# Three edits to a ten-stage transformer kernel on one core: the input's load, the close of the convolutions, and the squares of the neighbourhood attention

## The reference, cut to what matters

```python
x = first_block(x, ...)            # "mix" (two attentions) and a convolutional feed-forward
for i in range(4):                 # mixers: conv, nat, ret, conv
    h = rmsnorm(x, norm1_g[i])
    x = x + mixer_i(h)
    h = rmsnorm(x, norm2_g[i])
    x = x + conv_ffn(h, ...)

def conv_module(h, w_in, b_in, dw_w, dw_b, ln_g, ln_b, w_out):
    a, gt = jnp.split(h @ w_in + b_in, 2, axis=-1)
    u = a * jax.nn.sigmoid(gt)
    u = dwconv(u, dw_w, dw_b)      # depthwise, 31 taps
    u = layernorm(u, ln_g, ln_b)
    return jax.nn.silu(u) @ w_out

# nat_mixer: per head of 64 features
q = rmsnorm(qkv[:, :, 0], q_g) * (NAT_HEAD_DIM ** -0.5)
k = rmsnorm(qkv[:, :, 1], k_g)
```

## Time and profile before

| what | value |
|---|---|
| median of 3 runs | 1642.3 us (1642.21 to 1643.4) |
| the profiled execution, its own time | 1641.51 us |
| its span | 1639.4 us |
| PE busy | 1609.6 us (98%), 10544 matmuls |
| DVE busy | 1223.5 us (75%) |
| ACT busy | 897.9 us (55%) |
| POOL busy | 68.7 us (4%) |
| chunk 0's first matmul | at 11.61 us |
| last transposes of conv0, first matmul of its output chunk | 411.17 and 414.58 us |
| nat: first matmul of chunk 0, last sum of squares | 629.21 and 687.37 us |

### The profile page before, as it was taken

One profiled execution on the slowest core, in us unless ns is written; L12 is line 12 of the kernel. 1 busy time (PEld: TensorE's weight loads), 2 busy tenths in 40 slices (PEclk: granted clock), 3 DMA queues, 4 the chain that ended last, 5 costly groups with the idle time before them and its releaser, 6 DMA issues.

```text
span 1639.4 us, 28560 instructions
## 1 busy us (share of the span) xinstructions
PE 1609.6 (98%) x10544; PEld 1458.4 (89%) x10544; DVE 1223.5 (75%) x1842; ACT 897.9 (55%) x1178; POOL 68.7 (4%) x77
## 2 busy tenths in 40 slices
PE   8999999999999999999999999999999999999998
PEld 8888999978899998888999998877999987799997
DVE  5766878778687877865877786446787887878787
ACT  5575554565655546575554555444645556664553
POOL 0041000000000000020000033000100000000000
PEclk9999999999999999999999999999999999999999
DMA  7444545443655454422545455533554545345443
GB/s 287 132 152 166 205 167 194 176 162 121 238 190 187 179 204 151 158 104 103 201 160 194 188 181 192 192 128 140 182 201 182 181 178 180 135 150 202 180 181 126
DMA packets 41889, 284.13 MB, mean 173 GB/s; under 512 B 4992, under 2 KB 5120, under 8 KB 8928
## 3 DMA queue, kind: packets, MB, share of 16 engines
q1 hardware_dynamic: 39552, 273.90, 45.7%
q0 software_dynamic: 2272, 9.32, 1.6%
HBM read 282.16 MB, written 1.05 MB: 173 GB/s over the span
## 4 chain that ended last, share of the span: by engine, by line
PE 88%; DVE 8%; ACT 2%; issue 1%; DMA 1%; DVEq 0%; SPq 0%; ACTq 0%
PE bank L1863 15%; PE bank L1865 15%; PE bank L1864 15%; PE bank L1957 8%; PE bank L1958 8%; PE bank L1959 8%; PE bank L1909 4%; PE bank L1910 4%; PE bank L1911 4%; DVE w_lo L1057 1%; DVE arena L1338 1%; PE bank L2018 1%; DMA raw<-wstream 1%; PE bank L1845 1%; PE bank L2283 1%
## 5 line engine op out<-in xcount | busy, mean ns | idle before, releaser
L1863 PE MATMUL bank<-h_hi,w_hi 128*128 128x256 f32 x2220 | 636.3, 287 | 4.8 <-DVE w_lo L1057 2.6
L1864 PE MATMUL bank<-h_hi,w_lo 128*128 128x256 f32 x2220 | 630.8, 284 | 0.0
L1865 PE MATMUL bank<-h_lo,w_hi 128*128 128x256 f32 x2220 | 630.7, 284 | 0.0
L1863 PEld LDWEIGHTS bank<-h_hi,w_hi 128*128 128x128 f32 x2220 | 426.2, 192 | 12.1 <-issue 6.2
L1864 PEld LDWEIGHTS bank<-h_hi,w_lo 128*128 128x128 f32 x2220 | 426.2, 192 | 4.4 <-issue 1.4
L1865 PEld LDWEIGHTS bank<-h_lo,w_hi 128*128 128x128 f32 x2220 | 426.2, 192 | 0.8
L1365 DVE TENSOR_TENSOR w_lo<-raw,w_hi 128x2048 fp32r<-128x2048 f32 x145 | 327.6, 2285 | 1.6 <-ACT w_hi L797 1.6
L1057 DVE TENSOR_TENSOR w_lo<-raw,w_hi 128x2048 fp32r<-128x2048 f32 (+3 forms) x110 | 237.4, 2158 | 111.8 <-ACT w_hi L585 111.8
L785 ACT ACTIVATE arena<-arena,par 128x256 f32<-128x256 f32 x220 | 120.4, 595 | 358.0 <-DVE arena L1324 354.7
L797 ACT ACTIVATE w_hi<-raw 128x2048 fp32r<-128x2048 f32 x150 | 286.1, 1907 | 19.7 <-PE bank L1959 19.7
L1957 PE MATMUL bank<-w_hi,h_hi 128*128 128x512 f32 x632 | 248.1, 393 | 3.3 <-DVE h_lo L1663 1.8
(11 more groups left out here) (206 smaller groups left out, 1327.2 us busy)
## 6 DMA issues: line engine op xcount, KB each, us to landing
raw<-wstream SPq DMA_DIRECT2D x254, 1024.0 KB, 4.8
arena<-window_bias POOLq DMA_DIRECT2D x4, 768.0 KB, 7.3
arena<-dilated_bias POOLq DMA_DIRECT2D x8, 256.0 KB, 5.1
arena<-conv_rows POOLq DMA_DIRECT2D x2, 1024.0 KB, 4.8
raw<-wstream SPq DMA_DIRECT2D x6, 256.0 KB, 3.5
raw<-wstream SPq DMA_DIRECT2D x4, 384.0 KB, 3.4
cst<-consts SPq DMA_DIRECT2D x1, 1088.0 KB, 11.7
x<-x_in SPq DMA_DIRECT2D x2, 512.0 KB, 5.3
```

Of the source, the lines that this page charges most:

```text
L1863: nc.tensor.matmul(dst, w_parts[0], x_parts[0], start=start, stop=False, **kw)
L1864: nc.tensor.matmul(dst, w_parts[1], x_parts[0], start=False, stop=False, **kw)
L1865: return nc.tensor.matmul(dst, w_parts[0], x_parts[1], start=False, stop=stop, **kw)
```

## The change

**Start.** x comes in one transfer; chunk 2 is loaded ahead of the tables. The parts of chunk 1 are made in halves, with PE waiting for each half, and PE's idle transposes after `turn` are 20 instead of 8.

**Convolutions' close.** GpSimd makes the first half of chunk c0+10's low part, in four pieces of 256 columns, behind the last wave part. DVE's first half goes; its second half moves behind the second low part of the silu's output. PE's first output chunk waits for the two halves apart. The statistics of section 0 are cut in two: token half 0 ahead of the last `products`, half 1 behind. ACT makes the high part of chunk c0+11 ahead of the last `wave_parts`.

**Squares.** ACT copies the squares to a high part, GpSimd subtracts the low part, and PE sums with two float32r matmuls in place of one in float32. The ones are copied to float32r once. The first sum moves from the end of chunk 1 into chunk 2; the others keep their places.

```diff
@@ SP
-            sp.dma_start(x[:, :, 0:D // 2], x_rows[:, :, 0:D // 2]).then_inc(x_loaded, 16)
+            sp.dma_start(x[:, :, :], x_rows).then_inc(x_loaded, 16)
             sp.dma_start(cst[:, 0:FIRST], consts_in[:, 0:FIRST]).then_inc(consts_loaded, 16)
             sp.dma_start(par[:, 0:EARLY], params_in[:, 0:EARLY]).then_inc(consts_loaded, 16)
             sp.dma_start(raw[:, 0, 0:QUARTER], wstream[0, :, 0:QUARTER]).then_inc(quarter_full[0], 16)
-            sp.dma_start(x[:, :, D // 2:D], x_rows[:, :, D // 2:D]).then_inc(x_rest, 16)
...
             load(1)
+            load(2)
             sp.dma_start(par[:, EARLY:NP_], params_in[:, EARLY:NP_]).then_inc(tables_loaded, 16)
             sp.dma_start(cst[:, FIRST:NC_], consts_in[:, FIRST:NC_]).then_inc(tables_loaded, 16)
@@ GpSimd
-            def low_parts(c, piece):
+            def low_parts(c, piece, first_half=False):
...
-                for at in range(0, widths[c], piece):
+                for at in range(0, HALF if first_half else widths[c], piece):
...
-                last.then_inc(lo_done, 1)
+                last.then_inc(first_lows if first_half else lo_done, 1)
...
                 if name == "nat":
+                    for n in range(8):
+                        g = k["sq"]
+                        hi, lo = sq_parts(g)
+                        pool.wait_ge(sq_hi_done, n + 1)
+                        nc.gpsimd.tensor_tensor(lo, sq[:, g % 2, :], hi.bitcast(F32), ALU.subtract).then_inc(sq_lo_done, 1)
+                        k["sq"] += 1
                     for c in (13, 14):
                         low_parts(c0 + c, 512)
+                if name.startswith("conv"):
+                    k["conv"] += 1
+                    pool.wait_ge(wave_lo, 9 * k["conv"])
+                    low_parts(c0 + 10, 256, first_half=True)
@@ ACT
-                    split_hi(1, second=True)
+                    act.wait_ge(raw_full[1], 16)
+                    nc.scalar.activation(w_hi[:, 1, 0:HALF], raw[:, 1, 0:HALF], ACT.Copy).then_inc(half_hi, 1)
+                    nc.scalar.activation(w_hi[:, 1, HALF:CH], raw[:, 1, HALF:CH], ACT.Copy).then_inc(hi_done, 1)
...
                     y_evac_conv(0)
+                    split_hi(c0 + 11)
                     wave_parts(2)
                     y_evac_conv(1)
-                    split_hi(c0 + 11)
                     y_evac_conv(2)
...
                 elif name == "nat":
+                    nc.scalar.activation(half_ones_r, cc("half_ones", P), ACT.Copy).then_inc(half_set, 1)
...
                             squares([(pair(qk_n, c), 512, evac_done, k["evac"])])
+                            g = k["sq"] - 1
+                            act.wait_ge(sq_done, g + 1)
+                            nc.scalar.activation(sq_parts(g)[0], sq[:, g % 2, :], ACT.Copy).then_inc(sq_hi_done, 1)
@@ DVE
                     wave_parts(1)
+                    stats(0, (0,))
                     products(2)
                     wave_parts(2)
-                    stats(0)
+                    stats(0, (1,))
                     stats(1)
-                    half_lo_of(c0 + 10, 0)
                     stats(2)
...
-                    half_lo_of(c0 + 10, 1)
                     for t in range(8):
...
                         if t == 1:
+                            dve.wait_ge(first_lows, k["conv"])
+                            half_lo_of(c0 + 10, 1)
                             split_lo(c0 + 11)
@@ PE
                 if not k["x"]:
-                    keep_busy(8, bank[7])
+                    keep_busy(20, bank[7])
...
+                    if first_low and (a, q) == (1, ORDER[0]):
+                        pe.wait_ge(lo_done, c + 1)
...
+                    def split_sum(n):
+
+                        hi, lo = sq_parts(k["sq"])
+                        k["sq"] += 1
+                        if k["stat"]:
+                            pe.wait_ge(stat_read, k["stat"])
+                        pe.wait_ge(half_set, 1)
+                        pe.wait_ge(sq_lo_done, n + 1)
+                        nc.tensor.matmul(stat[:, 0:2 * S], half_ones_r, hi, start=True, stop=False)
+                        nc.tensor.matmul(stat[:, 0:2 * S], half_ones_r, lo, start=False, stop=True).then_inc(sum_done, 1)
+                        k["stat"] += 1
...
-                                          between=root_row if c == 1 else None)
+                                          between={1: root_row, 2: lambda: split_sum(0)}.get(c))
...
-                        if 1 <= c <= 8:
-                            sum_squares([512], half_ones)
+                        if 2 <= c <= 8:
+                            split_sum(c - 1)
```

More of the change, by code:

```diff
@@ L357, in flat, with sq_parts @@
             return view.rearrange("p a b -> p (a b)")
+        def sq_parts(g):
+            at = slice(8 + 2 * (g % 2), 10 + 2 * (g % 2))
+            return flat(h_hi[:, at, :]), flat(h_lo[:, at, :])
+        half_ones_r = h_hi[:, 12, 0:P]
         def turn_bank_conv(n):
@@ L461, in _ @@
             end = n_chunks // RING
-            for c in range(2, start * RING):
+            for c in range(RING, start * RING):
                 load(c)
@@ L529, in _ @@
                 if name == "mix":
+                    k["sq"] += 3
                     ones_columns(v_a)
@@ L1166, in prenorm @@
                 k["hlo"] += 8
-                split_lo(c0 + 1, second=True)
+                if c0 == 0:
+                    for part, ready, made in ((slice(0, HALF), (half_hi, 3), half_lo), (slice(HALF, CH), (hi_done, 2), lo_done)):
+                        dve.wait_ge(*ready)
+                        nc.vector.tensor_tensor(w_lo[:, 1, part], raw[:, 1, part], w_hi[:, 1, part].bitcast(F32), ALU.subtract)\
+                                 .then_inc(made, 1)
+                else:
+                    split_lo(c0 + 1, second=True)
                 token_root()
@@ L1599, in wave_parts, with stats @@
                             nc.vector.tensor_tensor(lo, src, hi, ALU.subtract).then_inc(wave_lo, 1)
-                    def stats(e):
+                    def stats(e, halves_=(0, 1)):
                         first, n = section(e)
                         dve.wait_ge(y_out, e0 + e + 1)
-                        for t in range(2):
+                        for t in halves_:
                             for at in range(first, first + n, GROUP):
@@ L1878, in feature_chunk @@
                     pe.wait_ge(*free)
-                if c:
+                if c > 1:
                     pe.wait_ge(lo_done, c + 1)
@@ L1886, in feature_chunk @@
                         pe.wait_ge(*((lo_done, 1) if m else (half_lo, t // 4 + 1)))
+                    if c == 1 and t == 0:
+                        pe.wait_ge(*((lo_done, 2) if m else (half_lo, 3)))
                     if wait_h is not None and m == 0:
@@ L1941, in sum_squares, with down_chunk @@
                 sums(for_sum, matrix, S if matrix is None else widths_[0], start, stop)
-            def down_chunk(c, slot_c, h0, first=False, last_=False, wait_h=(), free=None, between=None):
-                pe.wait_ge(lo_done, c + 1)
+            def down_chunk(c, slot_c, h0, first=False, last_=False, wait_h=(), free=None, between=None, first_low=None):
+                pe.wait_ge(*(first_low or (lo_done, c + 1)))
                 for a, q in [(a, q) for a in range(2) for q in ORDER]:
+                    if first_low and (a, q) == (1, ORDER[0]):
+                        pe.wait_ge(lo_done, c + 1)
                     if q == ORDER[0] and wait_h:
@@ L1962, in down_chunk, with out_chunks @@
                 last.then_inc(chunk_used, 1)
-            def out_chunks(c0, n, first_h, wait_h, free=None, between={}):
+            def out_chunks(c0, n, first_h, wait_h, free=None, between={}, first_low=None):
                 for i in range(n):
@@ L1968, in out_chunks @@
                                [(hlo_done, wait_h + 2 * i + 1), (hlo_done, wait_h + 2 * i + 2)],
-                               free if i == 0 else None, between.get(i))
+                               free if i == 0 else None, between.get(i), first_low if i == 0 else None)
             def score_pair(scores, g):
```

13 lines of the change are left out of this document (8 added, 5 removed).

## The result

The changed kernel took 1633.41 us by the median of five runs (1633.27 to 1634.14), the kernel before 1642.3 (five runs, 1641.76 to 1643.4): 8.9 us less, a ratio of 0.9946 with a 95% interval of 0.9935 to 0.9957. The forecast was 1636.7, with a range down to 1634.3. The sign was right; the gain was larger than the range allowed.

The account below looks back on a forecast made before the run. TensorE was busy 98% of the span, with DVE's chain ending last at all three edited places. Savings of 2 x 1.8 + 1.5 + 0.5 = 5.6 us gave 1642.3 - 5.6 = 1636.7 us, range 1634.3 to 1639.8.

Parts of the forecast that it names:

- Closes, 1.8 each: Close of conv0 and conv1: section 2's statistics start earlier and PE's output chunk no longer waits, 1.8 us saved each.
- PE's transposes (411.17, 2.5 us) ... end at 412.75 ... PE's output chunk starts at about 412.8: conv0's close: transposes end at 412.75 instead of 413.7, and the output chunk starts near 412.8 instead of 414.58.
- Section 2's output is then there at 406.73 + 0.35 = 407.1: conv0's close: statistics ahead of the last products make section 2's output 0.35 us later.
- It costs nothing: Convolutions' close: ACT's high part of chunk c0+11, 1.9 us, made earlier, at no cost.
- Squares, 1.5: nat: two float32r matmuls replace each float32 sum; DVE sets the pace, its chain begins 0.95 us later, 1.5 us saved.
- the fit by 0.1 us: nat: GpSimd's subtraction ends 1.3 us after the root's reading, DVE's next two-input step comes at 1.4 us.
- Squares give nothing: Rival in nat: the fit misses by 0.2 us, so each of seven roots slips by that; 1638.2 us, chance 0.16.
- Start, 0.5: Kernel's start: chunk 0 starts near 11.6 us again but at 2.4 GHz; 0.5 us saved.
- I take 0.5: Kernel's start: value taken between nothing and up to 1.3 us, depending on whether chunk 3 comes 1.2 us forward.
- the clock falls earlier: Rival at the start: 1.2 GHz during the transposes, chunk 0 about 2 us later, start -1.4; 1638.6 us, chance 0.12.
- slower rival: GpSimd holds DVE in nat and closes: roots 7.7 us apart, DVE ends 9.9 later, 6.6 behind PE's need; 1650.0 us, chance 0.04.

Follow-up runs that it names:

- nat_early: Changed kernel with nat's ACT work on the first chunk and the fourth chunk's high part ahead of its row-sum wait, first sum back at chunk 1's end: 1632.04 us.
- sub_twice: Changed kernel with each of GpSimd's eight subtractions of the squares in nat made twice: 1641.56 us, 7.9 more than the changed kernel.
- before_busy: Kernel before with more idle transposes: 36 for 20 behind a convolution's last inverse, 32 for 24 ahead of ffn0's and conv0's transposes: 1641.6 us against 1642.7.
- conv_only: Kernel before with only the edits of the two convolution closes: 1638.42 us against 1642.32, 3.9 less.

## Why the prediction was wrong, step by step

The sum had the main mechanisms that the traces show, but it was too small in three places, all in one direction: the closes by 0.8 us together, the start by 1.0, and the step from the trace to the median by 1.4, for which it had no term. With closes and start set right it gives 1642.3 - 7.5 = 1634.8, and with the missing step alone 1642.3 - 7.0 = 1635.3, both inside the range. Only the two together leave it.

**Closes, 1.8 each: 2.18 in the traces.** The links were right: free GpSimd pieces, section 2's statistics held only by their output, no wait ahead of the output chunk, the wave parts 0.32 us later (0.35 said). What failed is the step "PE's transposes (411.17, 2.5 us) ... end at 412.75 ... PE's output chunk starts at about 412.8": the 2.5 us are a busy time with a modelled end, and the stream takes 2.29. That is 0.3. The other 0.1 is the step "Section 2's output is then there at 406.73 + 0.35 = 407.1": it came 0.08 later and not 0.35, and by the rows that is because ACT's high part of chunk c0+11 no longer stood ahead of its copy. "It costs nothing" was said of that move; it gave something. A term mis-sized, by 0.4 a close.

**Squares, 1.5: 1.55.** The later beginning of DVE's chain (0.95 said, 0.86 measured), its pace, GpSimd's 2.6 us behind the low part and the fit by 0.1 us all came as worked out, and nat_early and sub_twice show from both sides that these are what the term rests on. "Squares give nothing" needed 0.2 us more of GpSimd's time; it had 0.14 to spare. That the term held to 0.1 us is partly luck, since its fit did.

**Start, 0.5: 1.3 in the trace and 0.24 more at ffn0, 2.2 alone by the median, 2.0 for x in one transfer.** This is the trace's largest mis-sized term, by 1.0. "I take 0.5" lay between nothing and 1.3, and the upper end came true. The 0.24, a shorter wait at ffn0 that goes with the halves, was not in the text at all. And both ends were read from one execution in which x's second half came early, at 9.53 us; in five traces of other kernels with the old load and order of x the transposes behind it start at 9.40 to 11.02. At the point that is 80.51 in the kernel before, the seven traces with the old load of x have PE at 80.51 to 81.45, the middle one at 80.91; the seven with the whole new start and 20 idle transposes at 78.88 to 79.73, the middle one at 79.38. That is 1.5 between the middle ones, though chunk 0 begins anywhere from 10.19 to 12.26 in the latter: its first matmul isn't what counts. A range drawn from one arrival of a transfer is no bound.

**The sum from trace to median.** The text took the difference of 0.8 us between the profiled execution and the median as a constant and subtracted the same 5.6 from both. It is not: in other executions the clock falls and x comes later, and the change removes both. The kernel before scattered over 3.1 to 4.6 us in sets of 15 to 33 runs (1.6 in the first five), the changed one over 0.5 and 0.9 in five each, and sub_twice, which has its start and closes, over 0.7 in ten. This part, some 1.4 us, had no term. How it divides is not settled: before_busy gives 1.1 to the clock by its median, with an interval that reaches to nothing, and conv_only, where the clock no longer falls at the closes either, gained 3.9 by its median and not more than its trace's 4.4. Its interval, 2.5 to 5.4 us, allows both.

**The rivals.** The clock fell in nat_early's profiled start (0.50 between 8 and 10 us, during the idle transposes), so "the clock falls earlier" does happen. Chunk 0 then began at 12.26 us, 1.5 later than in the changed kernel's trace, but PE was only 0.2 to 0.3 us later at mix's attention (79.53 against 79.21 and 79.34), where the prediction took 1.9. In nat in the changed kernel GpSimd never got in ahead of DVE's steps behind a root, which took 0.69 us each. Where it was made to, in sub_twice, the roots came 7.44 us apart in the mean, near the 7.7 of the slower rival; that rival's 9.9 and 6.6 us can't be worked out from the rows that the prediction names.

The sum again with what was measured: 2 x 2.2 + 1.55 + 1.5 = 7.5 in the trace, and 1.4 from the trace to the medians: 8.9.

## What to carry to other kernels

Where one engine's chain sets the pace, ask when the chain begins: moving ACT's work on the first squares and on one chunk's high part into its idle 3.2 us doubled what the squares gave (3.4 us against 1.55 in the traces). A gain that rests on 0.1 us of fit between two engines that exclude each other should be tried with the second one made longer, before something else makes it longer. And before adding terms from one profiled execution, look at the scatter of the runs: here they spread by 3 us and more, transfers and the clock differed from one trace to the next, and the change that shortened those waits gained more by the median than in the trace.

## What was not expected of the hardware

The clock's fall behind a wait of about 2 us happens in most executions and not in all. Six kernels that are alike at the closes, one trace each, had it in five at conv0 and in four at conv1; behind two waits of 0.95 and 0.96 us at ffn0 two of five had it. By the Trainium skill, TensorE: Matmul & The Clock Gate, "What's actually happening", an idle engine is throttled and activity releases it; the rows agree in kind. What a fall costs is set by what stands behind it: 1.5 us at ffn0, where PE's stream follows, 0.05 to 0.58 at a close, where ACT and DVE chains follow (transposes to the wait at 456.89: 45.72 us without a fall, 45.77 to 46.30 with one).
